# Tokens turned in pieces of two, two and four channel tiles, with the second weight unit prepared ahead of the second pieces and the high parts multiplied first

## What is computed

```python
h = rms_norm(x, norm_mix[l])              # x: (1, 512, 1024)
proj = h @ w_in[l]                        # w_in: (1024, 6656)
q_a, k_a, v_a, q_b, k_b, v_b, u_c, g_logits = jnp.split(proj, IN_SPLITS, axis=-1)
...                                       # attention A and B, pooling, gates
x = x + merged @ w_out[l]
h2 = rms_norm(x, norm_ffn[l])
x = x + conv_gated_mlp(h2, w_up[l], conv_w[l], conv_b[l], w_down[l])
```

## Time and profile before

| | |
|---|---|
| median of 3 runs | 816.08 us (815.91 to 817.07) |
| the profiled execution, its own time | 815.84 us |
| its span, first to last instruction | 814.2 us |
| PE busy | 807.6 us, 99% of the span |
| DVE, ACT busy | 638.9 us, 418.2 us |
| granted TensorE clock | 1.00 in the mean |

### The profile page before, as it was taken

One profiled execution on the slowest core, in us unless ns is written; L12 is line 12 of the kernel. 1 busy time (PEld: TensorE's weight loads), 2 busy tenths in 40 slices (PEclk: granted clock), 3 DMA queues, 4 the chain that ended last, 5 costly groups with the idle time before them and its releaser, 6 DMA issues.

```text
span 814.2 us, 11415 instructions
## 1 busy us (share of the span) xinstructions
PE 807.6 (99%) x3808; PEld 669.3 (82%) x3808; DVE 638.9 (78%) x944; ACT 418.2 (51%) x587; POOL 23.6 (3%) x38
## 2 busy tenths in 40 slices
PE   8999999999999999999999999999999999999998
PEld 6888888888888888888878888888888888888886
DVE  5958888867668675668688868777777788898797
ACT  6547676656645644334356564433443344566653
POOL 0010010000000060000000000000000000000000
PEclk9999999999999999999999999999999999999999
DMA  6342333312222224365637322666565555576455
GB/s 212 105 131 78 91 91 86 95 52 79 77 77 77 66 78 142 92 206 179 192 121 232 104 77 83 201 206 204 185 202 193 181 179 195 163 220 211 150 181 174
DMA packets 131071, 115.37 MB, mean 142 GB/s; under 512 B 6260, under 2 KB 109656, under 8 KB 129888
## 3 DMA queue, kind: packets, MB, share of 16 engines
q1 hardware_dynamic: 130048, 112.47, 44.0%
q0 software_dynamic: 672, 2.12, 1.0%
q10 hardware_dynamic: 320, 0.40, 0.2%
HBM read 101.31 MB, written 13.65 MB: 141 GB/s over the span
## 4 chain that ended last, share of the span: by engine, by line
PE 94%; DVE 3%; issue 1%; DMA 1%; ACT 0%; SPq 0%; DVEq 0%; ACTq 0%
PE ps L1829 29%; PE ps L1830 29%; PE ps L1831 29%; PE ps L1951 2%; PE ps L1942 2%; PE ps L1966 1%; PE ps L1965 1%; DMA x_in<-in_x_dram 1%; DVE suffix L1285 1%; DVE w_lo L1109 1%; PE ps L2147 0%; PE ps L1866 0%; DVE out_sb L1814 0%; PE ps L1925 0%; PE ps L1926 0%
## 5 line engine op out<-in xcount | busy, mean ns | idle before, releaser
L1829 PE MATMUL ps<-h_lo,w_hi 128*128 128x512 f32 x704 | 277.0, 393 | 0.1
L1830 PE MATMUL ps<-h_hi,w_hi 128*128 128x512 f32 x704 | 274.3, 390 | 0.0
L1831 PE MATMUL ps<-h_hi,w_lo 128*128 128x512 f32 x704 | 274.2, 390 | 0.0
L1109 DVE TENSOR_TENSOR w_lo<-w_raw,w_hi 128x1024 fp32r<-128x1024 f32 x104 | 128.2, 1232 | 68.0 <-ACT w_hi L620 33.8
L1829 PEld LDWEIGHTS ps<-h_lo,w_hi 128*128 128x128 f32 x704 | 132.2, 188 | 28.3 <-DVE w_lo L1109 0.7
L1831 PEld LDWEIGHTS ps<-h_hi,w_lo 128*128 128x128 f32 x704 | 132.2, 188 | 27.8
L1830 PEld LDWEIGHTS ps<-h_hi,w_hi 128*128 128x128 f32 x704 | 132.3, 188 | 26.1
L620 ACT ACTIVATE w_hi<-w_raw 128x1024 fp32r<-128x1024 f32 x72 | 76.3, 1059 | 139.6 <-PE ps L1831 139.5
L614 ACT ACTIVATE w_hi<-w_raw 128x1024 fp32r<-128x1024 f32 x32 | 33.9, 1060 | 62.7 <-PE ps L1831 59.6
L1677 DVE TENSOR_TENSOR conv_in<-ps,r_ffn 128x512 f32<-128x512 f32 x44 | 30.4, 690 | 22.5 <-PE ps L1831 22.2
L1028 ACT ACTIVATE conv_out<-conv_in,par 128x512 f32<-128x512 f32 x44 | 35.5, 807 | 9.7 <-DVE conv_in L1677 9.7
(11 more groups left out here) (283 smaller groups left out, 1356.5 us busy)
## 6 DMA issues: line engine op xcount, KB each, us to landing
w_raw<-in_w_in_dram SPq DMA_DIRECT2D x103, 256.0 KB, 3.1
w_raw<-in_w_up_dram SPq DMA_DIRECT2D x88, 256.0 KB, 3.2
raw_t<-in_w_down_dram SPq DMA_DIRECT2D x9, 1024.0 KB, 8.9
down_sums<-t_sum SPq DMA_DIRECT2D x9, 1024.0 KB, 5.7
w_raw<-in_w_down_dram SPq DMA_DIRECT2D x33, 256.0 KB, 3.0
w_raw<-down_sums SPq DMA_DIRECT2D x33, 256.0 KB, 3.8
raw_o<-in_w_out_dram SPq DMA_DIRECT2D x6, 512.0 KB, 4.8
w_raw<-down_sums SPq DMA_DIRECT2D x22, 128.0 KB, 2.9
```

Of the source, the lines that this page charges most:

```text
L1109: v.tensor_tensor(w_lo[:, slot, :], w_raw[:, slot, :], r32(w_hi[:, slot, :]), ALU.subtract)\
L1829: mm3(dst, l_hi, r_lo, start=start, stop=False, **kw)
L1830: mm3(dst, l_hi, r_hi, start=False, stop=False, **kw)
L1831: return mm3(dst, l_lo, r_hi, start=False, stop=stop, **kw)
```

## The change

Three things are changed at once.

- A tile of tokens is loaded, transposed and split in three pieces of two, two and four channel tiles, instead of two pieces of four. The four loads of the first pieces are 128 KB instead of 256 KB each, four loads of second pieces of 128 KB are new, and the third pieces (256 KB) follow. The second pieces use the other two places of the tile's PSUM bank (their transposes are still written with a wait for the first piece's low part); their landings are counted on `d_landed`, whose later users count 16 more.
- On PE the second pieces are transposed inside unit 0, before the products of tiles 2 and 3, and the third pieces inside unit 1, each after that tile's first product. Unit 1's `w_hi` and `w_lo` stay right behind the first pieces on ACT and DVE, so they now stand ahead of the second pieces.
- In unit 0 the order of a product's three matmuls becomes high by high, low by high (`xt_lo`, `w_hi`), high by low (`xt_hi`, `w_lo`) with a wait of its own ahead of each, instead of all waits ahead of the first (`first_products`).

```diff
@@ -272,7 +272,17 @@
 
             return ps[:, X_BANKS[t], :].rearrange("p (k c) -> p k c", c=P)
 
+        XG = (slice(0, 2 * P), slice(2 * P, 4 * P), slice(4 * P, 8 * P))
+        XK = ((0, 2), (2, 4), (4, 8))
+
+        def x_group_landed(t, g):
+            return (x_landed[t][0], d_landed[t], x_landed[t][1])[g]
+
         def x_split(buf, t, g):
+            return buf[:, slice(*XK[g]), t * P:t * P + P]
+
+        def x_group_turned(t, g):
+            return x_turned(t)[:, 2 * (g % 2):2 * (g % 2) + 2, :] if g < 2 else x_turned(t)
 
 
             return buf[:, 4 * g:4 * g + 4, t * P:t * P + P]
@@ -333,8 +343,9 @@
         def _(sp):
             def x_load(t, g):
 
-                c = slice(g * WB, g * WB + WB)
-                sp.dma_start(x_in[:, t, c], xw[:, t, c]).then_inc(x_landed[t][g], 16)
+
+                c = XG[g]
+                sp.dma_start(x_in[:, t, c], xw[:, t, c]).then_inc(x_group_landed(t, g), 16)
 
             def load(n, slot, halves):
 
@@ -359,6 +370,8 @@
             values(N_VA + 1, 1, V_A * P)
             for t in range(TT):
                 x_load(t, 1)
+            for t in range(TT):
+                x_load(t, 2)
             values(N_VA + 2, 2, V_A * P)
 
             sp.wait_ge(rows_zero, 1)
@@ -627,8 +640,8 @@
 
             def xt_split_hi(t, g):
 
-                a.wait_ge(xt_rest_done if g else xt_done, t + 1)
-                act(x_split(xt_hi, t, g), x_turned(t), ACT.Copy).then_inc(xt_hi_ready, 1)
+                a.wait_ge(xt_rest_done if g == 2 else xt_done, TT * (g % 2) + t + 1)
+                act(x_split(xt_hi, t, g), x_group_turned(t, g), ACT.Copy).then_inc(xt_hi_ready, 1)
 
             def values_hi(n, u):
 
@@ -651,8 +664,8 @@
 
             def square(t):
 
-                for g in range(2):
-                    a.wait_ge(x_landed[t][g], 16)
+                for g in range(3):
+                    a.wait_ge(x_group_landed(t, g), 16)
                 if t:
                     a.wait_ge(ssq_done, t)
                 act(squares[:, :], x_in[:, t, :], ACT.Square, accum_out=tok[:, 0, t:t + 1]).then_inc(ssq_done, 1)
@@ -664,10 +677,12 @@
             for t in range(1, TT):
                 xt_split_hi(t, 0)
             values_hi(N_VA + 1, 1)
+            for t in range(TT):
+                xt_split_hi(t, 1)
             square(0)
             square(1)
             for t in range(TT):
-                xt_split_hi(t, 1)
+                xt_split_hi(t, 2)
             values_hi(N_VA + 2, 2)
             square(2)
             square(3)
@@ -918,7 +933,7 @@
                 if m < 2 * NO:
                     a.wait_ge(osum_ready, s + 1)
                 elif u == 0:
-                    a.wait_ge(d_landed[s - NO], 32)
+                    a.wait_ge(d_landed[s - NO], 48)
                 if m < 4:
                     a.wait_ge(unit_done, N_OUT if m == 1 else N_OUT - 1)
                 else:
@@ -1038,7 +1053,7 @@
 
             def down_hi(m, e, u, use, wide=UNIT):
 
-                a.wait_ge(d_landed[2 * e + u], use * 32 + 64)
+                a.wait_ge(d_landed[2 * e + u], use * 32 + 80)
                 if isinstance(m, int) and m < 4:
                     a.wait_ge(unit_done, N_DOWN - 1 if m == 0 else N_DOWN)
                 else:
@@ -1120,7 +1135,7 @@
             def xt_split_lo(t, g):
 
                 d.wait_ge(xt_hi_ready, TT * g + t + 1)
-                v.tensor_tensor(x_split(xt_lo, t, g), x_turned(t), r32(x_split(xt_hi, t, g)), ALU.subtract)\
+                v.tensor_tensor(x_split(xt_lo, t, g), x_group_turned(t, g), r32(x_split(xt_hi, t, g)), ALU.subtract)\
                     .then_inc(xt_lo_ready, 1)
 
             def first_lo(i):
@@ -1155,8 +1170,10 @@
             values_lo(N_VA + 1, 1)
             for t in range(TT):
                 xt_split_lo(t, 1)
+            for t in range(TT):
+                xt_split_lo(t, 2)
             values_lo(N_VA + 2, 2)
-            d.wait_ge(xt_lo_ready, 2 * TT)
+            d.wait_ge(xt_lo_ready, 3 * TT)
             parts_added(0)
             parts_added(2)
 
@@ -1857,14 +1874,14 @@
 
             def x_transposes(t, g):
 
-                pe.wait_ge(x_landed[t][g], 16)
-                if g == 1:
-                    pe.wait_ge(xt_lo_ready, t + 1)
+                pe.wait_ge(x_group_landed(t, g), 16)
+                if g:
+                    pe.wait_ge(xt_lo_ready, TT * (g - 1) + t + 1)
                 if (t, g) == (2, 0):
                     pe.wait_ge(gmix_ready, 1)
-                for k in range(4 * g, 4 * g + 4):
+                for k in range(*XK[g]):
                     last = nc.tensor.transpose(x_turned(t)[:, k % 4, :], x_in[:, t, k * P:k * P + P], ident[:, :])
-                last.then_inc(xt_rest_done if g else xt_done, 1)
+                last.then_inc(xt_rest_done if g == 2 else xt_done, 1)
 
             def value_product(bank, k, t, c, slot):
 
@@ -1882,22 +1899,44 @@
                             last.then_inc(v_b_half, 1)
                 last.then_inc(unit_done, 1)
 
+            def first_products(kk, t):
+
+
+                bank, tk, c = V_A_BANKS[t], slice(t * P, t * P + P), slice(kk * WB, kk * WB + WB)
+                pe.wait_ge(xt_hi_ready, t + 1)
+                if t == 0:
+                    pe.wait_ge(hi_ready if kk else first_hi_ready, 1)
+                mm3(ps[:, bank, :], xt_hi[:, kk, tk], w_hi[:, 0, c], start=kk == 0, stop=False)
+                pe.wait_ge(xt_lo_ready, t + 1)
+                mm3(ps[:, bank, :], xt_lo[:, kk, tk], w_hi[:, 0, c], start=False, stop=False)
+                if t == 0:
+                    pe.wait_ge(lo_ready if kk else first_lo_ready, 1)
+                return mm3(ps[:, bank, :], xt_hi[:, kk, tk], w_lo[:, 0, c], start=False, stop=False)
+
             x_transposes(0, 0)
             warm(1)
             x_transposes(1, 0)
-            for t in range(TT):
-                pe.wait_ge(xt_lo_ready, t + 1)
-                for kk in range(2):
-                    if t == 0:
-                        pe.wait_ge(lo_ready if kk else first_lo_ready, 1)
-                    last = value_product(V_A_BANKS[t], kk, t, slice(kk * WB, kk * WB + WB), 0)
-                    if t == 0:
-                        x_transposes(kk + 2, 0)
+            first_products(0, 0)
+            first_products(1, 0)
+            x_transposes(2, 0)
+            first_products(0, 1)
+            x_transposes(3, 0)
+            first_products(1, 1)
+            for t in (2, 3):
+                x_transposes(2 * t - 4, 1)
+                first_products(0, t)
+                x_transposes(2 * t - 3, 1)
+                last = first_products(1, t)
             last.then_inc(unit_done, 1)
-            for t in range(TT):
-                x_transposes(t, 1)
-            values(N_VA + 1, V_A_BANKS, 1)
-            pe.wait_ge(xt_lo_ready, 2 * TT)
+            pe.wait_ge(lo_ready, N_VA + 2)
+            for kk in range(2):
+                for t in range(TT):
+                    pe.wait_ge(xt_lo_ready, TT + t + 1)
+                    last = value_product(V_A_BANKS[t], 2 + kk, t, slice(kk * WB, kk * WB + WB), 1)
+                    if kk == 0:
+                        x_transposes(t, 2)
+            last.then_inc(unit_done, 1)
+            pe.wait_ge(xt_lo_ready, 3 * TT)
             values(N_VA + 2, V_A_BANKS, 2)
             pe.wait_ge(rows_landed, 11 * 16)
             for t in range(2):
```

## The result

The changed kernel takes 818.48 us (median of 13 runs, 818.18 to 819.02), the kernel before 816.34 us (13 runs, 815.75 to 818.16). The ratio is 1.0025, with a 95% interval of 1.0018 to 1.0033: **slower by 0.25%, 2.1 us by the medians.** The profiled execution took 818.48 us of its own, with a span of 816.8, so 2.6 us more than the one profiled before.

The account below looks back on a forecast made before the run. PE's work plus its waits was taken to bound the kernel, with only waits able to move. Unit 2's low part 2.4 us later, less 0.4 of room, gave +2.0 on 815.84 (817.84; 818.1 by the median), stated as 817.9, range 816.3 to 819.1.

Parts of the forecast that it names:

- What bounds the kernel: Whole span: PE's work plus its waits; whatever the first 40 us gain or lose is not taken up later.
- The sum: Whole kernel: unit 1 starting at 13.9 gives +2.0 us; 817.84 by the profiled run, 818.1 by the median, stated as 817.9.
- the rival of pieces that don't come sooner: First loads: SP's issue time and ACT's separate queue hold the weights' landing at 7.1; 818.4 us, chance 0.25.
- the main case: Weights' landing near 6.6 us: time 817.3 to 818.3, elsewhere 817.3 to 818.6; chance 0.32.
- The landing L: Second half of unit 0's weights: lands at 6.6 us, between 6.2 and 7.1; before, about 7.12.
- Unit 1 at T = L + 7.3: PE: T, the start of unit 1, comes 7.3 us after landing L, at 13.9; comparable number before 14.07.
- the signs that the prediction named: Profile: right if unit 1 starts 13.5 to 14.4, q tile near 40.3; wrong if PE starts slower before 6 us.
- The second pieces: Unit 0: first lands at 9.2 to 9.8, wanted at 10.3, no stall; late rival up to 1 us, 819, chance 0.08.
- T + 6.5 for unit 2's `w_lo`: DVE begins unit 2's low part 6.5 us after unit 1 starts, at 20.4 against 18.02, 2.4 us later.
- The chain of 19.69 us: DVE from unit 2's `w_lo` to the first `h_lo`: the same 19.69 us follow in the same order, ending at 40.1.
- The room of 0.6 us less 0.2: PE at the q tile: 0.6 us of room less 0.2 for a restart, so 2.4 us late becomes 2.0.
- The formula T - 11.9: Loss in general from unit 1's start: +1.6 us at 13.5, +2.5 at 14.4, +3.0 at 14.9.

Follow-up runs that it names:

- e1: Changed kernel with unit 2's high parts on ScalarE ahead of the third pieces' copies and its low parts on VectorE ahead of their subtractions; 817.68 us, ratio 1.0013.
- e2: Changed kernel with two of VectorE's four sums of high and low parts moved ahead of the third pieces' subtractions, unit 2 still late; 817.47 us, ratio 1.0012.
- e3: Changed kernel with the edits of e1 and e2, and the last two sums also ahead of the norm factor's work; 816.59 us, ratio 1.0002.
- e5: Changed kernel with the 16 transposes of the third pieces in one go ahead of unit 1; 817.39 us, ratio 1.0010.
- e6: Changed kernel with unit 0's three matmuls per product in the old order, behind all their waits; 818.95 us, ratio 1.0028.
- e8: Kernel before with only VectorE's first sum of parts moved ahead of the second pieces' subtractions; 816.28 us, ratio 0.9999.
- e4: Kernel before with two of VectorE's sums made twice, ahead of unit 2's low parts; 818.48 us, ratio 1.0025.
- e7: e3 with the second half of unit 0's weights loaded by SyncE behind tile 1's first piece instead of by ScalarE's queue; 816.19 us, ratio 0.9999.

## Why the prediction was right

- *What bounds the kernel.* Shown. What the first 40 us lost stood in the time in full: q tile 2.47 later, span 2.6 longer.
- *Luck in the number.* The +2.0 us of the forecast agree with +2.1 by the medians because two errors nearly cancel: T was 0.5 too low, and the execution profiled before, from which the loss was counted, was an early one (see *The sum*). By the time alone the result sits on the rival of pieces that don't come sooner (T = 14.4, 818.4) and above the 817.3 to 818.3 of the main case, to which the prediction gives 818.6 as its upper end in another place. It takes the profiles to tell the two apart: the landing did come sooner, and T was late for another reason.
- *The landing L.* Predicted 6.6, in this profile 6.64. But `e1`, `e2`, `e3` and `e5`, with the same code up to there, had 6.96, 6.97, 6.84 and 7.13, and the kernel before 7.15, 7.54 and 7.78 in its variants. With `e6` (7.25) the mean of the six with the changed start is 7.0, and of the three with the old start 7.5. So the agreement to 0.04 us is luck, the landing comes forward by half a microsecond rather than the 0.9 that the bytes alone would give, and in the mean my value was 0.4 low.
- *Unit 1 at T = L + 7.3.* Predicted 13.9, measured 14.39, the step with the largest error. It was not the landing that held PE in this execution: its matmuls stood 0.43 us apart up to 8.3 us, and 0.23 from 8.7 on. I had reckoned with full speed from tile 1's transposes on, as in the execution profiled before. Where the speed came early (`e1`), the landing at 6.96 held PE, with 0.7 us of idle time, and unit 1 started at 14.38 all the same, 0.1 above L + 7.3. Two limits of about the same size stood one behind the other. PE's timeline of `e1`:

```profile
6.71 0.39 PE L1914 MATMUL ps<-w_lo,xt_hi 128*128 128x512 f32 x1
7.83 0.47 PE L1909 MATMUL ps<-w_hi,xt_hi 128*128 128x512 f32 x1 [0.72 <-ACT w_hi L663]
```

  With T at 14.39 PE was 0.3 us behind the 14.07 of before, not 0.2 ahead. Of the signs that the prediction named, `w_hi` of unit 2 at 19.59 is just outside its 18.6 to 19.5, and one listed under wrong came true in part: a lower speed of PE's first products, though up to 8.3 us.
- *The second pieces.* Right: no stall. The transfers issued from 4.4 to 5.0 us landed 4.4 us later (median), so at about 9.0; PE wanted the first at 10.7, ahead of its fifth product (the prediction's "ninth" is a slip). The row, of the changed kernel's transfers:

```profile
x_in<-in_x_dram SPq DMA_DIRECT2D x2, 128.0 KB, 4.4
```

  The Trainium skill (DMA: Bandwidth & Descriptors, section Bandwidth) advises batching transfers to a MiB. That a halved piece would save next to nothing was a misreading of it: a straight line between the page's 0.95 us for 64 KB and 6.15 us for 1 MB makes a halved piece 0.7 us shorter (an estimate). In this filled queue the two 128 KB pieces took 4.4 us to land, where a 256 KB piece at that place took 7.0. As 512 KB less stood ahead of them, no run here tells what the size of a piece alone does.
- *T + 6.5 for unit 2's `w_lo`.* 14.39 + 6.5 = 20.9, measured 20.95.
- *The chain of 19.69 us.* 19.67 here. The room of 0.6 us less 0.2: the chain is 2.93 late, the q tile 2.47, so 0.46 was taken up, where I had 0.4. The formula T - 11.9 gives 2.49 for T = 14.39, and the stops lay where they were forecast: 0.9 at unit 2 (0.8), 0.1 at each of the next two (0.1 to 0.3), 0.7 at the q tile (0.8).
- *The sum.* +2.0 forecast, +2.1 by the medians, +2.6 between the two profiles. The profiled execution of before was an early one: other kernels with its start began unit 1 at 16.13 and 16.35 (15.74 there), with landings 0.4 and 0.6 us later. That fits the profiles' differing by more than the medians: `e8`, which began unit 1 0.4 us later than the execution profiled before, took 816.28 us to its 815.84.
- *Which part did what.* Shown by `e1` to `e5`: unit 2's lateness and the chain behind it are the loss, the interleaved transposes account for about 1 us of it, and high parts first gives back 0.5 (the time alone leaves this open, the profiles support it). That ScalarE's squares starting later makes up the rest was argued from the timeline, not tried.

## What to carry to other kernels

An edit that spreads work out on the busiest engine also spreads out the engines that follow it: ask for the last item, not the first, and what is queued behind it. Here PE was 99% busy and the loss came from VectorE, 78% busy, since its work after unit 2 was one unbroken chain with 0.6 us to spare. Before such a reorder, add up the time for which a helper engine works without a gap up to the next hand-over, and move what it can do early (here the sums) into the idle time ahead of it.

## What the runs showed of the hardware

With the same code up to there, TensorE's first matmuls changed from 0.43 to 0.23 us apart at different times in different executions: before 6.1 us in `e1` and `e2`, between 8.3 and 8.7 in the changed kernel, `e3` and `e5`. In `e6` and `e7`, whose starts differ a little, it was near 7.2 and at 7.9. The profile's clock row says 1.00 throughout these stretches, so the spacing of the matmuls is the better witness; the row of PE's window from 6 to 8 us in the changed kernel, all of it slow:

```profile
6.00:8.00 2.00, 2.00 (x7) 1.00 0.96 333
```

The second half's product began at 7.86 in the changed kernel and at 7.83 in `e1`, once held by the slow matmuls and once by the landing. So a gain of either alone in the first 9 us of this kernel can be lost to the other; `e7`, with both earlier, began unit 1 0.2 us sooner.

The weights that are the first to hold PE landed between 6.6 and 7.3 us in the six profiles with the changed loads, and between 7.1 and 7.8 us in the three with the old ones. A single execution does not give such a landing to better than 0.3 us, and the half microsecond between the two means rests on these nine.
